# Spreading the row factors of two norms over all partitions: by a store and a load instead of diagonal blocks and matmuls

## The reference

```python
def rms_norm(x, g):
    xf = x.astype(jnp.float32)
    y = xf * lax.rsqrt(jnp.mean(xf * xf, axis=-1, keepdims=True) + EPS)
    return (y * g.astype(jnp.float32)).astype(x.dtype)

def layer_a(h, g_norm, w_in, ...):
    u = rms_norm(h, g_norm)
    proj = u @ w_in
    ...
    return h + jnp.concatenate([y_rnn, y_mem], axis=-1) @ w_out

# reference(): layer A, then keys and values from its residual stream, then layer B
h = layer_a(...)
k_sb, v_sb = jnp.split(rms_norm(h, kv_norm) @ w_kv, 2, axis=-1)
h = layer_b(...)      # begins with rms_norm(h, norm_b) @ w_in_b
return rms_norm(h, final_norm)
```

## Time and profile before

| | |
|---|---|
| median of 3 runs | 1477.69 us (1477.19 to 1477.70) |
| the profiled execution | 1477.59 us |
| its span | 1475.4 us |
| PE busy | 1461.9 us, 99% |
| DVE busy | 994.3 us, 67% |
| ACT busy | 715.7 us, 49% |
| POOL busy | 122.3 us, 8% |
| DMA | 243 GB/s in the mean |

### The profile page before, as it was taken

One profiled execution on the slowest core, in us unless ns is written; L12 is line 12 of the kernel. 1 busy time (PEld: TensorE's weight loads), 2 busy tenths in 40 slices (PEclk: granted clock), 3 DMA queues, 4 the chain that ended last, 5 costly groups with the idle time before them and its releaser, 6 DMA issues.

```text
span 1475.4 us, 18186 instructions
## 1 busy us (share of the span) xinstructions
PE 1461.9 (99%) x6850; PEld 1221.0 (83%) x6850; DVE 994.3 (67%) x1302; ACT 715.7 (49%) x1063; POOL 122.3 (8%) x184
## 2 busy tenths in 40 slices
PE   8999999999999999999999999999999999999997
PEld 7888888888888888888888888888888888888886
DVE  5764558465586896856568676566566556578977
ACT  5764453544544655764325654433433433455465
POOL 0001111111110000000010001210111111100000
PEclk9999999999999999999999999999999999999999
DMA  9796788787885887477999866777887878879853
GB/s 329 238 347 214 160 210 250 186 212 165 203 247 161 320 313 260 162 259 271 334 372 351 293 221 211 229 232 177 241 240 191 236 202 220 244 233 315 314 198 143
DMA packets 155262, 357.96 MB, mean 243 GB/s; under 512 B 7745, under 2 KB 25153, under 8 KB 151105
## 3 DMA queue, kind: packets, MB, share of 16 engines
q1 hardware_dynamic: 105040, 206.50, 40.8%
q0 software_dynamic: 29376, 102.77, 28.4%
q10 hardware_dynamic: 20784, 47.88, 9.0%
HBM read 310.98 MB, written 113.25 MB: 288 GB/s over the span
## 4 chain that ended last, share of the span: by engine, by line
PE 95%; DVE 2%; ACT 1%; DMA 1%; issue 0%; SPq 0%; ACTq 0%; DVEq 0%
PE main L2018 23%; PE main L2019 23%; PE main L2020 23%; PE aux L2018 5%; PE aux L2019 5%; PE aux L2020 5%; PE aux L2349 2%; PE aux L2295 2%; PE aux L2291 2%; PE aux L2293 2%; PE main L2295 1%; PE main L2291 1%; PE main L2293 1%; PE aux L2338 1%; DMA w_raw<-in_w_out_b 1%; PE aux L2141 0%
## 5 line engine op out<-in xcount | busy, mean ns | idle before, releaser
L2018 PE MATMUL main<-act_hi,w_hi 128*128 128x512 f32 x1216 | 475.7, 391 | 0.0
L2020 PE MATMUL main<-act_hi,w_lo 128*128 128x512 f32 x1216 | 473.8, 390 | 0.0
L2019 PE MATMUL main<-act_lo,w_hi 128*128 128x512 f32 x1216 | 473.6, 389 | 0.0
L2020 PEld LDWEIGHTS main<-act_hi,w_lo 128*128 128x128 f32 x1216 | 228.2, 188 | 48.1
L2019 PEld LDWEIGHTS main<-act_lo,w_hi 128*128 128x128 f32 x1216 | 228.3, 188 | 46.6
L2018 PEld LDWEIGHTS main<-act_hi,w_hi 128*128 128x128 f32 x1216 | 228.4, 188 | 46.4
L1257 DVE SCALAR_TENSOR_TENSOR w_lo<-w_raw,gains,w_hi 128x512 fp32r<-128x512 f32 x188 | 128.8, 747 | 121.6 <-ACT w_hi L659 121.4
L659 ACT ACTIVATE w_hi<-w_raw,gains 128x512 fp32r<-128x512 f32 x188 | 120.5, 713 | 143.8 <-PE main L2020 114.7
L1249 DVE TENSOR_TENSOR w_lo<-w_raw,w_hi 128x1024 fp32r<-128x1024 f32 x88 | 104.1, 1222 | 94.2 <-ACT w_hi L654 93.9
L654 ACT ACTIVATE w_hi<-w_raw 128x1024 fp32r<-128x1024 f32 x88 | 88.4, 1057 | 152.2 <-issue 89.4
L2018 PE MATMUL main<-w_hi,act_hi 128*128 128x512 f32 x352 | 137.8, 391 | 2.1 <-DVE w_lo L1369 1.8
(11 more groups left out here) (300 smaller groups left out, 2040.9 us busy)
## 6 DMA issues: line engine op xcount, KB each, us to landing
w_raw<-in_w_in_a SPq DMA_DIRECT2D x32, 1024.0 KB, 6.8
w_raw<-in_w_in_b SPq DMA_DIRECT2D x32, 1024.0 KB, 8.0
weight_sums<-in_w_out_a POOLq DMA_DIRECT2D x48, 512.0 KB, 7.0
weight_sums<-in_w_out_b POOLq DMA_DIRECT2D x48, 512.0 KB, 7.5
weight_sums<-weight_sums POOLq DMA_DIRECT2D x32, 512.0 KB, 6.3
w_raw<-weight_sums SPq DMA_DIRECT2D x16, 1024.0 KB, 7.1
work<-weight_sums SPq DMA_DIRECT2D x16, 1024.0 KB, 6.4
w_raw<-in_w_mem_kv SPq DMA_DIRECT2D x15, 1024.0 KB, 5.2
```

What stands on the lines that cost most here:

```text
L2018: TE.matmul(o, a[0], b[0], start=first, stop=False)
L2019: TE.matmul(o, a[0], b[1], start=False, stop=False)
L2020: return TE.matmul(o, a[1], b[0], start=False, stop=final)
```

## The change

Both times the diagonal blocks, the matmuls with ones and the copy from PSUM go. In their place GpSimd's queue stores the 128 x 4 factors to a row of 512 in HBM (`rstd_dram`), waits until that has landed, and loads the row into all 128 partitions of `rstd_bc` at once. The last instruction of `inverse_root` signals GpSimd (`rstd_made`), and DVE waits for the load (`rstd_loaded`) where it waited for PE.

```diff
+    rstd_dram = nc.dram_tensor("rstd_scratch", [2, T], F32, kind="Internal").ap()
...
-        diag = four(7)
...
+            def spread_rstd(n):
+                pool.wait_ge(rstd_made, n + 1)
+                pool.dma_start(rstd_dram[n].rearrange("(t p) -> p t", p=P), rstd[:],
+                               allow_slow_non_contiguous=True).then_inc(rstd_stored, 16)
+                pool.wait_ge(rstd_stored, 16 * n + 16)
+                pool.dma_start(rstd_bc[:], rstd_dram[n:n + 1].broadcast_to([P, T])).then_inc(rstd_loaded, 16)
...
             pool.wait_ge(sumsq_ready, NMB + NT)
+            spread_rstd(0)
             for n in range(4):
...
                     load_sums(0)
                     load_sums(1)
+                    spread_rstd(1)
                     for step in range(KQ):
                         store_sums(step)
...
-                ch.link(V.tensor_tensor(r, r, a, ALU.mult))
+                if made is None:
+                    ch.link(V.tensor_tensor(r, r, a, ALU.mult))
+                else:
+                    V.tensor_tensor(r, r, a, ALU.mult).then_inc(rstd_made, 1)
+                    dve.wait_ge(rstd_made, made)
...
-            def rstd_rows(n):
-
-                inverse_root(n, rstd)
-                for t in range(NT):
-                    last = V.tensor_scalar(diag[:, t, 0:P], ident[:], rstd[:, t:t + 1], None, ALU.mult)
-                last.then_inc(diag_ready, 1)
-
             def rstd_row_out(n):
-                dve.wait_ge(bc_done, n)
-                ch.link(V.tensor_copy(rstd_bc[:], aux[:, 3, :]))
+                dve.wait_ge(rstd_loaded, 16 * n)
...
-                    rstd_rows(2)
+                    inverse_root(2, rstd, made=1)
...
-                    rstd_rows(3)
+                    inverse_root(3, rstd, made=2)
...
-            def rstd_row(n):
-                pe.wait_ge(diag_ready, n)
-                for t in range(NT):
-                    last = TE.matmul(aux[:, 3, P * t:P * t + P], ones[:], diag[:, t, 0:P], start=True, stop=True)
-                last.then_inc(bc_done, 1)
...
-                slab(G_A, j, "T", {2: lambda: rstd_row(1)} if j == 3 else {})
+                slab(G_A, j, "T")
...
-                if j == 3:
-                    hooks = {0: lambda: rstd_row(2)}
```

More of the change, by code:

```diff
@@ L359, in trunk @@
         rms_ready = sem("rms_ready")
-        diag_ready = sem("diag_ready")
-        bc_done = sem("bc_done")
+        rstd_made = sem("rstd_made")
+        rstd_stored = sem("rstd_stored")
+        rstd_loaded = sem("rstd_loaded")
         kmt_done = sem("kmt_done")
@@ L1319, in bank, with inverse_root @@
                     dve.wait_ge(bank_done, 3 * G + b - 7)
-            def inverse_root(n, dst, k=4):
+            def inverse_root(n, dst, k=4, made=None):
                 dve.wait_ge(rms_ready, n)
```

## The result

The changed kernel took 1484.89 us (median of 6 runs, 1483.05 to 1488.61). The kernel before took 1477.7 us beside it (6 runs, 1477.0 to 1477.94). The ratio is 1.0049 [1.0039, 1.0059], with its 95% interval: slower by 7.2 us, where 1.84 us less was forecast. The profiled execution took 1488.61 us, with a span of 1486.9 us. It is the longest of its six runs, so its terms add up to more than the 7.2 us.

A forecast was written before the change was run, and what follows sets the result against it. PE was taken to bound the kernel, busy 1461.9 of 1475.4 us. Dropping the diagonal blocks saves 1.84 us, all else hidden: 1477.59 - 1.84 = 1475.75, as a median 1475.85 us; range 1475.1 to 1478.4.

The forecast's parts named there:

- the price of the store: Both places: the store of the factors takes 3.9 us, from the nearest row, a load of 128 pieces of 256 bytes.
- 10.3 us for both: First place, bound case: store and load at 10.3 us each, so the row lands at 146.4 and costs 4.9 us.
- rival 1: Second place: the row misses its deadline and PE waits for bank 0; chance 0.14 below 4.8 us of stall, 0.07 above.
- Rival 2: First place's row or the gate weights land late as transfers meet otherwise; 1.7 us stall, time 1477.6; chance 0.07.
- the 4.6 us for the row's load: Both places: the 256 KB load of the row takes 4.6 us, the least of the queue's 768 KB loads.
- The queue at the second place: The store's packets stand behind GpSimd's four 768 KB loads until 673.1; row there at 680.4, 2.1 us before the deadline.
- it costs 1 us per us: Second place: from 682.5 on, each us the row is late costs PE 1 us.
- The 1.84 us of the diagonal blocks: PE, both places: dropping the float32 matmuls saves 0.92 us each, together 1.84 us, all on the path.
- The deadlines: The row must be in SBUF at 141.5 at the first place and 682.5 at the second, or PE waits.
- what DVE dropped: Both places: four products with the identity (0.88 us) and the PSUM copy (0.69 us) go, worth nothing.
- Rival 3: PE meets a later wait that doesn't move, as at the tail, so no gain shows; time 1477.7, chance 0.05.

The follow-up runs named there:

- the repeated run: The changed kernel itself, unaltered, measured again beside the version with 16-byte pieces and one copy: 1487.14 us (5 runs), 1.0065 of the kernel before.

## Why the prediction was wrong

**The step that failed** is the price of the store. I wrote that no row shows a store of 512 pieces of 4 bytes, and took 3.9 us from the nearest row, a load of 128 pieces of 256 bytes. On an idle queue it took 9.1 to 10.5 us, and behind the four loads 11.0 to 12.1 us. My upper bound for any of these transfers was 10.3 us, and the bound case, "10.3 us for both" at the first place with a cost of 4.9 us, was nearest to what came: 9.5 + 8.4 us, a stall of 3.0 us. I had named it and given it no chance of its own. The mechanism is rival 1's, at both places instead of one; I gave it 0.21 at the second. Rival 2 had a late row at the first place, with 0.07, but from transfers that meet otherwise and not from the store's own price.

**What the price consists of.** In the changed kernel, the store's 32 packets on GpSimd's queue move until 131 us, and the landing is at 137.2 us. Some 6 us of the 9.5 us pass after its last packet. SyncE's 1 MB load, issued at 125.70, has its last packet before 131 us too and lands only at 136.7. In that time little else moves (windows of the changed kernel, at the first place):

```profile
129.00:131.00 2.00, 2.00 (x11) 1.65 (x10) 0.00 (x0) 0.00 (x0) 0.00 (x0) 1.00 0.65 240
131.00:133.00 2.00, 2.00 (x11) 1.65 (x10) 0.00 (x0) 0.09 (x1) 0.00 (x0) 1.00 0.00 0
133.00:135.00 2.00, 2.00 (x11) 1.65 (x10) 1.26 (x2) 2.00 (x4) 0.00 (x0) 1.00 0.23 70
135.00:137.00 2.00, 2.00 (x10) 1.67 (x9) 1.47 (x3) 0.47 (x1) 0.00 (x0) 1.00 0.43 98
```

A quiet stretch alone is no sign: in the version with one copy 129 to 131 us is empty too, for want of work, but the sums and gate weights issued then move at 172 and 315 GB/s. Here the gate weights are issued on ScalarE's queue at 133.14 and 133.63, and 70 to 98 GB/s flow until 137. The run with the sums late and nothing else is the fairest to compare, since there too the gate weights have the engines almost to themselves:

```profile
133.00:135.00 2.00, 2.00 (x11) 1.65 (x10) 2.00 (x4) 1.10 (x2) 0.00 (x0) 1.00 0.85 253
```

They land there after 2.9 and 3.2 us, and in the changed kernel after 5.7 and 7.9 us. SyncE's two 1 MB loads at this place land after 11.0 and 11.2 us, where they took 7.1 and 7.0 us, and 5.5 and 6.1 us with the sums late; at the second place two such loads take 15.6 and 9.2 us instead of 11.7 and 5.0. That is the second half of the failed step: the 4.6 us for the row's load. At the first place it was issued 0.4 to 1.3 us behind SyncE's second 1 MB load and just ahead of three sums, with the gate weights still under way, and took 8.4 to 9.1 us. With 16-byte pieces it was issued 5 to 7 us earlier, ahead of that 1 MB load, and took 3.6 to 3.9 us. How much of the difference is the store's after-effect, and how much the 1 MB load that it now met, isn't separated. At the second place it took 5.0 to 5.6 us: close to my figure.

**The queue at the second place** was right. The same 16-byte store takes 3.7 us at the first place and 6.4 to 7.7 us at the second, so its place behind the four loads costs some 3 to 4 us; in all four such runs it lands 0.2 us behind the fourth load. The rule of the Trainium skill (DMA: Bandwidth & Descriptors, Queues, rings and completion order), that one ring's descriptors are taken in order, agrees with these numbers. With the store at 16 bytes and one copy, the row was there 12.1 us after the factors were final, where I had 13.5 us (666.9 to 680.4). The error was not the queue but the landing.

The Trainium skill (DMA: Bandwidth & Descriptors, Anatomy of one DMA) gives such a transfer a fixed cost of about 2.0 us and bytes beyond it, by its fit; an estimate from it is about 2 us for 2 KB. The 16-byte store at 3.7 us is 1.7 us above that, the 4-byte store at 9.5 us is 7.5 us above it. The measurement decides, and this figure of the Trainium skill would have misled further than the row that I used.

**The clock** was a missing term. Of a stall I had written that it costs 1 us per us. At six of the seven stalls at the rows (3.3, 3.4, 3.5, 3.5, 4.0 and 4.8 us) the granted clock fell to 0.50, for some 3 to 7 us. Only at the 3.0 us of the changed kernel's first place it stayed at 1.00. The fall can come after PE has started again: at the second place of the repeated run PE starts at 693.48, and the windows show 0.91 from 694 to 695 us and then

```profile
695.00:696.00 1.00, 1.00 (x4) 0.74 (x3) 1.00 (x3) 0.63 (x1) 0.00 (x0) 0.50 0.00 0
```

By PE's starts beside those of the kernel before, such a stretch costs 1.5 to 2.9 us on top of the stall. It also came behind the 2.2 us at the gates with the additional 4-byte store, and did not come behind the 1.9 us at the gates of the repeated run. This may be part of why the changed kernel's runs lie further apart, 1483.05 to 1488.61, than those of the kernel before; only the profiled executions show their clock. What decides between these stalls is open.

**What held.** The 1.84 us of the diagonal blocks: with the row in time, the version with 16-byte pieces shows no gap where they stood, and is 2.6 us faster in the measurement that is clear of noise and 1.0 us in the other. The deadlines: the first bank was wanted when I said, less the shift of the start, and what DVE dropped gained nothing. Rival 2: waits of 0.4 to 2.2 us at the gates and the output weights, where I had sized it at 1.7 us. They differ between two profiles of the same kernel: the changed one has 1.3 us at the output weights and no row for the gates in the first, and 1.9 us at the gates in the second. Rival 3 fell.

**What stays open.** Why a store of 4-byte pieces lands so late, and why other queues are held up meanwhile, no row shows. The pieces of neighbouring partitions lie side by side in HBM in all these stores, so that smaller pieces are also closer together; 4-byte pieces far apart weren't tried, and would tell whether it is the size or the closeness. Sizes between 4 and 16 bytes, and above, weren't tried; nor was a 4-byte store with no other transfer about.

## What to carry to other kernels

A chain of small transfers is priced by its landing, so before it takes the place of on-chip work, have a row for a store of that very shape; a few bytes are not a small price. Lay a small array out so that each partition writes one run, even if that mixes the order, and undo the mix by one on-chip copy behind the load, not by a stepped read in each of the 76 consumers. And where a stall of TensorE is only "a few us too late", keep room in the range for a clock that falls behind it.

## What the runs showed of the hardware

- A store to HBM in pieces of 4 bytes lands after 9.1 to 10.5 us on an idle queue, with 512 pieces or 128; in pieces of 16 bytes it takes 3.6 to 3.8 us, with 128 pieces or 512.
- It lands some 6 us or more after its last packet (6.3 us in the changed kernel), and meanwhile other transfers are held up: 28 and 21 GB/s in two windows where the same kernel with 16-byte pieces has 240 and 377, and 12.6 us for a 1 MB load of another queue that takes 6.4 us there.
- On SyncE's queue, behind a 1 MB load, such a store landed after 14.3 us, some 5.5 us of them after its last packet.
- A product of 128x512 in float32 takes 1.05 us on DVE with one operand read at a step of four elements, and 0.69 us without; a copy that reads so takes 0.61 us.
- When PE stood still for 3.3 to 4.8 us in the midst of dense work, the granted clock fell to 0.50 (1.2 GHz) in six of six cases, for some 3 to 7 us. It fell once at 2.2 us, and stayed at 1.00 at 3.0 us and at 1.9 us (one case each).
